# Second expert product by column halves, half of each pair's scatter and the next pair's gather inside its down stage, and a one-queue opening with idle matmuls

## The chip, the cores and the metric

One NeuronCore of one Trainium2 chip runs the kernel. The metric is the device time of a launch in microseconds (us), lower is better. TensorE (PE) multiplies, VectorE (DVE) and ScalarE (ACT) do the elementwise work and empty PSUM, GpSimd (POOL) does little, SyncE (SP) issues nearly all DMAs. SBUF holds the data, PSUM has eight banks of 128 x 512 f32 in which products are summed. Everything is float32; a matmul instruction shows in the trace as two MATMUL records, so counts in the trace are twice those of the program.

## The reference

For 256 tokens of width 1024: three token mixers (a gated linear recurrence, an mLSTM and a gated delta rule) from one input projection `x @ w_in`, merged by gates and projected; a layer norm; a mixture of 32 experts, four for each token; a second layer norm.

```python
x = layer_norm(DN_ALPHA * x + token_mixers(x, ...), ln1_g, ln1_b)
top_val, top_idx = top_k(x @ router_w + router_b, 4); gate = softmax(top_val)
# for each expert e and its tokens:
hdn = x[tok] @ w1[e] + b1[e]                     # 1024 -> 2 x 1024
act = min(glu, 7) * sigmoid(1.702 * glu) * (clip(lin, -7, 7) + 1)
y   = act @ w2[e] + b2[e]                        # 1024 -> 1024
out[tok] += gate * y
x = layer_norm(DN_ALPHA * x + out, ln2_g, ln2_b)
```

## The kernel before

**The mixers (0 to 400 us).** The input lies turned (features on partitions) in `XT`; the projection weights come as 50 pieces of 1 MB or 0.5 MB (`weight_stream`) into three buffers `WB`. Products are called `gq` (query, key, value of the delta rule), `lx`, `ly`, `mq` and so on; `proj` makes one (L589). The first, `gq0`, is in `first_proj` (L628): its input and its weights come in four quarters, the weights by SP (L403), the input by ACT (L1109), and PE begins when the first quarter of both has landed. `small` (L635) follows, then `gq1` to `gq5`. DVE begins when `planes`, a table of constants that ACT loads fifth, has landed.

**The experts (405 us to the end).** Experts are taken in 16 pairs; of each expert up to 64 tokens, so that a pair fills the 128 partitions of an output as two column tiles (`a` = 0, 1). The weights of a pair are 24 chunks of 1 MB: 8 for the first half of the hidden width (`up(0, c)`), 8 for the second (`up(1, c)`, both L972), 8 for the product back (`down(c)`, L990). SP loads them two at a time (a step, 2 MB) into eight places, and waits for `chunk_used` before it reuses one (`load_turn`, L393); steps that fit beforehand are loaded during the mixers. The last step of a pair of pairs comes in two halves (L508). What PE does besides, in a pair: `bias` (L965), `turn_hidden` (L981, after DVE's `hidden`), `turn_gates` (L999) which turns the gate-weighted one-hot table, `gather` (L902), two halves, which collects the rows of the next pair by a product with a one-hot table `ONE`, and `scatter` (L890), which adds the pair's result `YS` to the output sums in PSUM banks 4 to 7. ACT's `gathered` copies each gathered half to `XE`, and ACT and DVE each copy half of `YS`.

**The order.** It is written out by hand: each engine runs its program in order and waits on semaphores. In pair `i` before, after two chunks of the up stage PE scatters pair `i-1` (both halves), then, around chunk 4, turns the gates of pair `i` and gathers for pair `i+1`; the down stage holds chunks and `turn_hidden` alone. The first pair has the gates and the gather of pair 1 in its down stage (`prepare`). From the fifth turn on the pairs run in a loop on the device. After the last pair: ACT and DVE copy `YS`, PE scatters both halves (3.43 us), DVE makes the statistics (L1793, L1796), subtracts the mean (L1807), ACT scales (L1378), POOL adds (L560), SP stores (L524 to L528).

## Time and profile before

| | us |
|---|---|
| median of 3 runs | 1332.62 (1331.07 to 1334.09) |
| the profiled execution: its time | 1331.97 |
| its span, first to last instruction | 1330.1 |
| PE busy | 1274.4 (96%) |
| DVE busy | 341.7 (26%) |
| DMA, share of the 16 engines, 500 to 1300 us | 1.01 |
| chain that ended last: PE, DMA, DVE | 74%, 24%, 1% |

The chain is followed back from the last instruction to whatever released each step. PE's share counts an engine that is nearly always busy, so the shares alone do not tell which of PE and DMA sets the time of a stage; the stretches do.

### The profile page before, as it was taken

What the parts mean: (1) busy time and instruction counts of PE and PEld (TensorE: products, weight loads), DVE (VectorE), ACT (ScalarE), POOL (GpSimd) and SP (SyncE); (2) the same over time, 40 slices, a digit from 0 to 9 for tenths busy, and PEclk for the clock granted to TensorE, in tenths of its full rate; (3) what the DMA queues carried; (4) which work ended last, traced back from release to release, by engine and by line L of the source; (5) the groups of instructions that cost most, each with busy time, mean ns of one, the idle gap of its engine ahead of it and who ended that gap; (6) DMA issues with size and microseconds to landing.
All of it is one profiled execution on the core that took longest, in us unless ns stands there. A gap on an engine that the chain in (4) does not pass through costs nothing.

```text
span 1330.1 us, 17352 instructions
## 1 busy us (share of the span) xinstructions
PE 1274.4 (96%) x7404; PEld 697.3 (52%) x7404; DVE 341.7 (26%) x746; ACT 157.3 (12%) x267; POOL 16.4 (1%) x19
## 2 busy tenths in 40 slices
PE   8999999999999999999999989999998999999896
PEld 7888788888884444343443434334343433334342
DVE  3868571221134211211112010120211111021113
ACT  1441630011012000000000000000000000000001
POOL 0000200000000000000000000000000000000001
PEclk9999999999999999999999999999999999999998
DMA  7645225535788999999999999999999999999995
GB/s 247 227 143 150 96 98 215 187 103 180 297 354 343 406 409 427 429 424 429 427 427 427 426 429 426 427 427 426 428 428 427 431 427 427 429 429 427 428 430 233
DMA packets 48685, 463.87 MB, mean 349 GB/s; under 512 B 11568, under 2 KB 13400, under 8 KB 16888
## 3 DMA queue, kind: packets, MB, share of 16 engines
q1 hardware_dynamic: 42072, 459.19, 83.8%
q10 hardware_dynamic: 6560, 3.89, 1.0%
q8 instruction: 43, 0.70, 0.2%
q14 instruction: 10, 0.08, 0.0%
HBM read 461.60 MB, written 1.47 MB: 348 GB/s over the span
## 4 chain that ended last, share of the span: by engine, by line
PE 74%; DMA 24%; DVE 1%; issue 0%; ACT 0%; POOL 0%; POOLq 0%; SPq 0%; DVEq 0%
PE ps L972 24%; PE ps L589 20%; DMA ring<-expert_w 14%; DMA mix<-expert_w 9%; PE ps L990 8%; PE ps L890 4%; PE ps L902 4%; PE ps L965 3%; PE ps L825 2%; PE ps L607 2%; PE ps L599 1%; PE ps L981 1%; PE ps L628 1%; PE ps L999 1%; PE ps L615 0%
## 5 line engine op out<-in xcount | busy, mean ns | idle before, releaser
L972 PE MATMUL ps<-ring,mix 128*64 128x512 f32 x1536 | 343.8, 593 | 0.1
L589 PE MATMUL ps<-mix 128*128 128x256 f32 x1248 | 273.7, 380 | 2.2 <-DVE ring L1621 2.2
L589 PEld LDWEIGHTS ps<-mix 128*128 128x128 f32 x1248 | 235.7, 190 | 35.5 <-issue 3.7
L972 PEld LDWEIGHTS ps<-ring,mix 128*64 128x64 f32 x1536 | 108.2, 137 | 196.5 <-issue 191.0
L990 PE MATMUL ps<-ring,mix 128*64 128x512 f32 x752 | 171.4, 595 | 26.0 <-DMA ring<-expert_w 26.0
L990 PEld LDWEIGHTS ps<-ring,mix 128*64 128x64 f32 x752 | 53.5, 137 | 129.7 <-issue 100.8
L972 PE MATMUL ps<-mix 128*64 128x512 f32 x512 | 115.7, 594 | 3.5 <-DMA mix<-expert_w 3.2
L1913 DVE TENSOR_SCALAR mix<-ps 128x512 f32<-128x512 f32 x32 | 22.1, 692 | 374.6 <-PE ps L972 374.6
L1922 DVE COPY mix<-ps 128x512 f32<-128x512 f32 x32 | 22.1, 692 | 245.5 <-PE ps L981 245.5
L972 PEld LDWEIGHTS ps<-mix 128*64 128x64 f32 x512 | 35.9, 137 | 74.3 <-issue 66.3
L990 PE MATMUL ps<-mix 128*64 128x512 f32 x272 | 61.6, 593 | 5.3 <-DMA mix<-expert_w 5.3
L890 PE MATMUL ps<-mix 128*64 128x512 f32 x272 | 61.3, 592 | 0.8 <-DVE mix L1928 0.8
L902 PEld LDWEIGHTS ps<-mix 128*64 128x64 f32 x1024 | 57.5, 137 | 8.6 <-issue 8.6
L1361 ACT ACTIVATE mix<-mix 128x512 f32<-128x512 f32 x32 | 20.2, 630 | 348.9 <-DVE mix L1913 348.9
L902 PE MATMUL ps<-mix 128*64 128x128 f32 x1024 | 61.2, 273 | 0.0
L965 PE MATMUL ps<-mix 128*64 128x512 f32 x252 | 59.6, 592 | 0.0
L990 PEld LDWEIGHTS ps<-mix 128*64 128x64 f32 x272 | 20.8, 137 | 43.8 <-issue 42.4
L1928 DVE COPY mix<-ps 128x512 f32<-128x512 f32 x16 | 11.1, 692 | 123.5 <-PE ps L990 123.5
L890 PEld LDWEIGHTS ps<-mix 128*64 128x64 f32 x272 | 19.4, 137 | 40.0 <-issue 38.3
L981 PEld LDWEIGHTS ps<-mix 128*64 128x64 f32 x512 | 30.1, 137 | 18.3 <-issue 18.3
L1366 ACT COPY mix<-ps 128x512 f32<-128x512 f32 x16 | 9.4, 586 | 243.7 <-PE ps L990 243.7
L965 PEld LDWEIGHTS ps<-mix 128*64 128x64 f32 x252 | 18.3, 137 | 35.1 <-issue 35.1
(271 smaller groups left out, 747.4 us busy)
## 6 DMA issues: line engine op xcount, KB each, us to landing
ring<-expert_w SPq DMA_DIRECT2D x141, 2048.0 KB, 31.8
mix<-expert_w SPq DMA_DIRECT2D x39, 2048.0 KB, 33.6
mix<-stream_w SPq DMA_DIRECT2D x42, 1024.0 KB, 4.9
mix<-expert_w SPq DMA_DIRECT2D x20, 1024.0 KB, 28.5
mix<-stream_w SPq DMA_DIRECT2D x8, 512.0 KB, 3.8
ring<-expert_w SPq DMA_DIRECT2D x4, 1024.0 KB, 6.5
mix<-stream_w SPq DMA_DIRECT2D x4, 256.0 KB, 5.5
mix<-x_turned ACTq DMA_DIRECT2D x4, 256.0 KB, 6.4
```

Of the source, the lines that this page charges most:

```text
L589: ins = mm(o[:, m * S:(m + 1) * S], w[:, c, m * P:(m + 1) * P], rhs[:, c, :], start=(m == 0 and c == 0), stop=(c == nk - 1), skip_group_ch ...
L607: ins = mm(o[0:lhs.shape[-1], lo:hi], lhs, rhs, start=True, stop=True, skip_group_check=True)
L825: ins = mm(o[:, d * GW:(d + 1) * GW], MG[:, c, t * P:(t + 1) * P], w[:, c, :], start=(d == pieces[0] and c == 0), stop=(c == KD - 1), skip ...
L890: ins = mm(PS[64 * a:64 * a + 64, 4 + 2 * t + h, :], gates[:, t * P + 64 * a:t * P + 64 * a + 64], rows[:, h * 512:(h + 1) * 512], start=f ...
L902: ins = mm(PS[64 * a:64 * a + 64, bank, c * P:(c + 1) * P], X1[:, t, k:k + 64], ONE[:, t, :], start=(c == 0 and t == 0), stop=(t == NT - 1 ...
L965: mm(PS[64 * a:64 * a + 64, bank + g, :], PICK[:, 2 * g + f, a, :], B1R, start=True, stop=False, skip_group_check=True)
L972: ins = mm(PS[64 * a:64 * a + 64, bank + g, :], XE[j][:, c, 64 * a:64 * a + 64], w[:, a * D + g * 512:a * D + g * 512 + 512], start=False, ...
L981: ins = mm(PS[64 * a:64 * a + 64, bank, c * P:(c + 1) * P], HID[:, c * P + 64 * a:c * P + 64 * a + 64], ident, start=True, stop=True, skip ...
L990: ins = mm(PS[64 * a:64 * a + 64, bank + h, :], HT[:, c // 4, c % 4, 64 * a:64 * a + 64], w[:, a * D + h * 512:a * D + h * 512 + 512], sta ...
L1361: A(SIG, GLU, ACT.Sigmoid, scale=SWIGLU).then_inc(E("sig_ready"), 1)
L1913: ts(GLU, PS[:, bank, :], LIMIT, None, ALU.min).then_inc(E("glu_ready"), 1)
L1922: nc_v.tensor_copy(HT[:, n[1], :, :], PS[:, bank, :].rearrange("p (q n) -> p q n", q=4)).then_inc(E("ht_ready"), 1)
```

## The change

1. **Opening.** Input and `gq0` weights are laid together in `first_w`, four quarters of 512 KB with 4 KB rows, and all come by SP, followed by `small_w` and, with no wait, the weights of `gq1` and `gq2`; that of `gq3` waits for `planes`. ACT issues its small loads after the fourth quarter and `planes` after `small_w`. DVE fills a 128 x 128 tile `IDLE` with ones first of all, and PE multiplies it by itself eight times (`WARM`) before `first_proj`, into a bank that nothing reads.
2. **Places.** The quarters lie where half a prefetch place lay: what was loaded as one half of step 7 early is now one half of step 4, and step 7 comes whole after the last projection.
3. **`down(k)`** takes two rows of blocks for one 512-column half: chunks 0, 1 (left) and 2, 3 (right) of the first hidden half, 4, 5 (left) and 6, 7 (right) of the second. The number and shape of its matmuls and of its bytes is the same. The left half of the result is whole after chunk 5.
4. **Scatter.** The left half (`scatter_half(0)`) goes between chunks 6 and 7 of the pair's own down stage, the right half (`scatter_half(1)`) into the up stage of the next pair, after two chunks. After the last pair the right half alone is left; DVE makes the statistics of the left half before it copies the right.
5. **Gather.** `turn_gates` and both halves of `gather` go from the up stage to the down stage one pair sooner than it, around chunk 4: pair `i` turns its gates and gathers for pair `i+1` in its own down stage. This holds for the last pair, too.

```diff
+            pe.wait_ge(E("idle_ready"), 1)
+            for n in range(WARM):
+                mm(PS[:, 7, 0:P], IDLE, IDLE, start=True, stop=True, skip_group_check=True)
...
+                sp.dma_start(area(MIX, 24 + 4 * k, 1024), first_w[k]).then_inc(E(f"first_in{k}"), 16)
+            sp.dma_start(WSM, small_w).then_inc(E("wsm_in"), 16)
...
-                if n == 1:
-                    sp.wait_ge(E("first_in2"), 32)
-                if n == 2:
-                    sp.wait_ge(E("wsm_in"), 16)
+                if n == 3:
+                    sp.wait_ge(E("planes_in"), 16)
...
                 if name == "br02":
-                    load_half(PLACES[6][:, 0:2 * D], 7, 0, "steps_in6")
+                    load_half(PLACES[4][:, 2 * D:], 4, 1, "steps_in4")
...
                 if name == "br22":
-                    load_steps(4, 0, 4)
+                    load_half(PLACES[4][:, 0:2 * D], 4, 0, "steps_in4")
...
-            load_half(PLACES[6][:, 2 * D:], 7, 1, "steps_in6")
+            load_steps(7, 0, 6)
...
+            def scatter_half(h, event, each, first=False):
+
+                for t in range(NT):
+                    for a in range(2):
+                        ins = mm(PS[64 * a:64 * a + 64, 4 + 2 * t + h, :],
+                                 GTS[:, t * P + 64 * a:t * P + 64 * a + 64], YS[:, h * 512:(h + 1) * 512],
+                                 start=first, stop=False, skip_group_check=True)
...
-                def down(c, bank):
-                    w = chunk(2 * KD + c)
-                    for h in range(2):
+                def down(k, bank):
+                    w = chunk(2 * KD + k)
+                    f, h, both = k // 4, k // 2 % 2, k % 2
+                    for c in (2 * both, 2 * both + 1):
...
+                gather(0, two + 1)
                 pe.wait_ge(E("ht_ready"), 2 * i + 2)
-                for c in range(4, KF):
-                    down(c, one)
+                turn_gates(two)
+                down(4, one)
+                pe.wait_ge(E("gt_ready"), i + 1)
+                gather(1, two)
+                if first:
+                    gates_of_all()
+                down(5, one)
+                down(6, one)
...
+                pe.wait_ge(E("ys0_ready"), i + 1)
+                scatter_half(0, "acc0_done", False, first)
+                down(7, one)
...
-            pe.wait_ge(E("ys_ready"), rounds * (2 * NPAIR))
-            scatter("acc_done")
+            pe.wait_ge(E("ys1_ready"), rounds * NPAIR)
+            scatter_half(1, "acc1_done", True)
```

**PE, the end of the loop and what follows it**, the last pair's down stage. Before (`L990` down, `L981` turn_hidden, `L890` scatter):

```order
L990 MATMUL ps<-ring,mix 64x512 x12
L981 MATMUL ps<-mix 64x128 x8
L990 MATMUL ps<-ring,mix 64x512 x12
L990 MATMUL ps<-mix 64x512 x4
L959 ISA
L990 MATMUL ps<-mix 64x512 x4
L1089 ISA
L1089 COMPARE_AND_BRANCH
L1092 REGISTER_ALU
L890 MATMUL ps<-mix 64x512 x8
```

The same place now (`L1001` down, `L991` turn_hidden, `L912` gather, `L1010` turn_gates, `L900` scatter_half):

```order
L1001 MATMUL ps<-ring,mix 64x512 x4
L1071 REGISTER_ALU
L912 MATMUL ps<-mix 64x128 x16
L1010 MATMUL ps<-mix 64x128 x4
L1001 MATMUL ps<-ring,mix 64x512 x4
L912 MATMUL ps<-mix 64x128 x16
L1001 MATMUL ps<-ring,mix 64x512 x4
L1001 MATMUL ps<-mix 64x512 x4
L900 MATMUL ps<-mix 64x512 x4
L969 ISA
L1001 MATMUL ps<-mix 64x512 x4
```

Two gathers, the turned gates and half a scatter have moved in between the last five chunks; behind the loop stand four matmuls (`L900`, half a scatter) where eight stood.

**PE, the up stage of pair 1** (the second pair). Before (`L965` bias, `L972` up, `L999` turn_gates, `L902` gather):

```order
L965 MATMUL ps<-mix 64x512 x4
L972 MATMUL ps<-ring,mix 64x512 x8
L890 MATMUL ps<-mix 64x512 x8
L972 MATMUL ps<-ring,mix 64x512 x8
L999 MATMUL ps<-mix 64x128 x4
L902 MATMUL ps<-mix 64x128 x16
L972 MATMUL ps<-ring,mix 64x512 x4
L902 MATMUL ps<-mix 64x128 x16
L972 MATMUL ps<-ring,mix 64x512 x4
```

Now (`L975` bias, `L982` up, `L900` scatter_half):

```order
L975 MATMUL ps<-mix 64x512 x4
L982 MATMUL ps<-ring,mix 64x512 x8
L900 MATMUL ps<-mix 64x512 x4
L982 MATMUL ps<-ring,mix 64x512 x16
L982 MATMUL ps<-mix 64x512 x8
```

The eight chunks of the stage stand with four matmuls between them where they stood with 8 + 4 + 16 + 16.

## Rows read from the trace of the kernel before

**Rows 1.** Stretches: us, busy time of each engine (records), PEclk, DMA share, GB/s

```profile
393.00:401.00 8.00, 8.00 (x56) 7.18 (x54) 3.18 (x14) 0.96 (x2) 0.00 (x0) 1.00 0.43 136
...
478.00:482.00 4.00, 4.00 (x22) 1.38 (x20) 0.00 (x0) 0.00 (x0) 0.00 (x0) 1.00 0.85 283
...
500.00:700.00 200.00, 200.00 (x1234) 81.11 (x1230) 35.16 (x77) 12.94 (x23) 0.00 (x0) 1.00 1.01 427
700.00:1300.00 600.00, 566.82 (x3380) 225.94 (x3378) 95.17 (x204) 34.54 (x61) 0.00 (x0) 1.00 1.01 428
```

**Rows 2.** The chain that ended last, late part: start us, us, what

```profile
1264.32 3.43 PE ps L890 x16
...
1271.19 0.44 PE ps L999 x8
1271.62 1.75 PE ps L902 x32
1273.37 1.72 PE ps L972 x8
...
1278.73 30.63 DMA ring<-expert_w
```

**Rows 3.** Waits of PE, 0 to 400 us: who waited for whom, us, times, longest

```profile
PE ps L589 <- DVE ring L1621: 2.2, 1, 2.2
```

**Rows 4.** Timeline, opening: start us, us, engine, line, operation, [idle before <-releaser]

```profile
0.75 1.91 SPq L403 DMA_DIRECT2D mix<-stream_w  x4
...
5.12 9.13 PE L628 MATMUL ps<-mix 128*128 128x256 f32 x32 [5.12 <-DMA mix<-x_turned]
...
19.79 0.06 DVE L1407 MEMSET mix<- 128x1 f32 x1 [19.79 <-DMA mix<-planes]
```

**Rows 5.** The chain again, at 92 us

```profile
92.38 6.91 PE ps L589 x32
```

**Rows 6.** Stretches of the opening, PE alone: us, PE busy (records), PEclk, DMA share, GB/s

```profile
6.00:7.00 1.00, 1.00 (x4) 1.00 0.94 328
...
10.00:11.00 1.00, 1.00 (x6) 1.00 0.91 323
```

**Rows 7.** DMA issues: line, count, KB each, median us from issue to landing

```profile
mix<-stream_w SPq DMA_DIRECT2D x8, 512.0 KB, 3.8
```

**Rows 8.** Timeline of DVE at 91 us

```profile
91.18 1.29 DVE L1501 TENSOR_TENSOR ring<-ps,mix 128x512 f32<-128x512 f32 x2 [4.23 <-PE ps L615]
```

**Rows 9.** Timeline of PE in pair 1

```profile
471.46 1.92 PE L902 MATMUL ps<-mix 128*64 128x128 f32 x32
```

**Rows 10.** Timeline, last pair and end, all engines

```profile
1304.49 1.94 PE L990 MATMUL ps<-ring,mix 128*64 128x512 f32 x8 [1.15 <-DMA ring<-expert_w]
...
1306.26 1.04 PE L981 MATMUL ps<-mix 128*64 128x128 f32 x16
...
1307.13 1.89 PE L990 MATMUL ps<-ring,mix 128*64 128x512 f32 x8
...
1309.49 3.65 PE L990 MATMUL ps<-ring,mix 128*64 128x512 f32 x16 [0.47 <-DMA ring<-expert_w]
...
1316.62 0.69 DVE L1928 COPY mix<-ps 128x512 f32<-128x512 f32 x1 [8.57 <-PE ps L990]
...
1317.36 3.65 PE L890 MATMUL ps<-mix 128*64 128x512 f32 x16 [0.78 <-DVE mix L1928]
...
1318.49 0.70 DVE L1793 BATCH_NORM_STATS2 mix<-ps 128x6 f32<-128x512 f32 x1 [1.18 <-PE ps L890]
...
1320.15 0.21 DVE L1796 BATCH_NORM_AGGREGATE mix<-mix 128x2 f32<-128x12 f32 x1
...
1322.09 1.43 DVE L1793 BATCH_NORM_STATS2 mix<-ps 128x6 f32<-128x512 f32 x2 [0.15 <-DVE mix L1803]
...
1323.32 2.35 POOL L560 TENSOR_TENSOR mix<-mix 128x1024 f32<-128x1024 f32 x1 [1172.67 <-ACT mix L1378]
...
1326.12 1.10 POOL L560 TENSOR_TENSOR mix<-mix 128x384 f32<-128x384 f32 x1 [0.46 <-ACT mix L1378]
```

More of the change, by code:

```diff
@@ L883, in _, with scatter @@
             out_proj("wo11b", 1, 1, (1,), count_first)
-            def scatter(event, gates=GTS, rows=YS, first=False):
+            def scatter(event, gates, rows):
                 for t in range(NT):
@@ L891, in scatter @@
                                      gates[:, t * P + 64 * a:t * P + 64 * a + 64], rows[:, h * 512:(h + 1) * 512],
[L892 to L894 removed]
+                                     start=False, stop=False, skip_group_check=True)
+                        ins.then_inc(E(event), 1)
+            def scatter_half(h, event, each, first=False):
[4 more added lines that the diff above has]
+                                 start=first, stop=False, skip_group_check=True)
+                    if event and (each or t == NT - 1):
+                        ins.then_inc(E(event), 1)
             def gather(half, bank):
@@ L1041, in pair @@
                     if second:
-                        pe.wait_ge(E("bank_free5"), bank_total[5])
-                        pe.wait_ge(E("gt_ready"), 1)
-                        pe.wait_ge(E("xe_ready"), 4)
-                    pe.wait_ge(E("ys_ready"), 2 * i)
-                    scatter(None, first=second)
-                    up(0, 2, one)
-                    up(0, 3, one)
-                if not first:
-                    pe.wait_ge(E("xe_ready"), 2 * i + 2)
-                    turn_gates(two)
-                    pe.wait_ge(E("onehot"), i + 2)
-                    gather(0, two + 1)
-                    up(0, 4, one)
-                    pe.wait_ge(E("gt_ready"), i + 1)
-                    gather(1, two)
-                    for c in range(5, KD):
+                        for b in (5, 7):
+                            pe.wait_ge(E(f"bank_free{b}"), bank_total[b])
+                    pe.wait_ge(E("ys1_ready"), i)
+                    scatter_half(1, None, False, second)
+                    for c in range(2, KD):
                         up(0, c, one)
-                    pe.wait_ge(E("xe_ready"), 2 * i + 4)
                 bias(1, two)
@@ L1106, in _ @@
             A = nc_s.activation
-            for k in range(QUARTERS):
-                first, last = KD // QUARTERS * k, KD // QUARTERS * (k + 1)
-                act.dma_start(XT[:, first:last, :], x_turned[:, first:last, :]).then_inc(E(f"first_in{k}"), 16)
-            act.dma_start(WSM, small_w).then_inc(E("wsm_in"), 16)
+            act.wait_ge(E(f"first_in{QUARTERS - 1}"), 16)
             act.dma_start(VC, vectors).then_inc(E("vec_in"), 16)
             act.dma_start(SC[:, 32:34], row_bias).then_inc(E("bias_in"), 16)
-            act.wait_ge(E(f"first_in{QUARTERS - 1}"), 16)
+            act.wait_ge(E("wsm_in"), 16)
             act.dma_start(CM, planes.rearrange("p (k n) -> p k n", n=P)).then_inc(E("planes_in"), 16)
@@ L1356, in turn_act @@
                     first = isinstance(i, int) and i == 0
-                    if not first:
-                        prepared(i, 1 - j, (two, two + 1, two))
                     for f in range(2):
```

106 lines of the change are left out of this document (50 added, 56 removed).

## The prediction, written before the changed kernel ran

> **What bounds the kernel now.** I read the stretches first, then the chain, then the timeline at three places: the opening, pairs 0 and 1, and the end. The stretches show three regimes [rows 1]. Up to 400 us PE is busy nearly all the time and the DMAs are not. From 500 to 700 us both are full: PE 200.00 of 200, DMA share 1.01 at 427 GB/s. From 700 us on PE has gaps (566.82 of 600) and the DMAs have none (1.01, 428 GB/s). So in the expert stage the weights decide: PE needs less for a pair than the DMAs do. A chunk of 1.049 MB at 427.6 GB/s is 2.45 us, a pair of 24 chunks 58.9 us. PE's pair is 24 chunks at 1.72, two biases at 1.72, a scatter of 3.43, two gathers at 1.75, gates 0.44 and two turns of the hidden values at 0.87 (1306.26 to 1307.13): 53.8 us [rows 2, 10]. Up to 700 us PE eats what was loaded beforehand, then it waits for each step. The chain says the same: one of its last pieces is a DMA of 30.63 us, up to the middle of the last down stage [rows 2].
>
> Two things follow. PE work saved or moved inside a pair in the middle is worth nothing. The end comes as: the time at which the stream of loads starts to run full, plus bytes over rate, plus every stretch in which the load queue runs dry, plus what stands after the last loads. The change is priced at these four.
>
> **The opening.** The stream runs full from about 405 us, when PE begins to free places, so what PE wins in the mixers moves everything behind it. PE starts at 5.12 and `first_proj` takes 9.13 us for 32 records [rows 4]; the same 32 records elsewhere take 6.91 [rows 5]. The stretches tell why: 4 records touch a microsecond from 6 to 7, and 6 from 10 to 11 [rows 6]. PEclk reads 1.00 in both, so the column does not show it; the pace of the records does: first the lower level (1.2 GHz), later the upper (2.4). A record of 256 columns takes 6.91/32 = 0.216 us on the upper, 0.43 on the lower, so 9.13 us are about 10 slow records and 22 fast ones: 4.4 us of work at the lower level, 2.2 us lost.
>
> The ones: 8 matmuls, 16 records of half the columns, 0.215 us each if slow, 3.4 us. They need only DVE's fill, so I estimate a start at 1.0 us (the first DMAs are issued at 0.75) and an end at 4.4. The first quarter, 512 KB on one queue, is of a size that lands 3.8 us after issue in the stream [rows 7]: 4.55 instead of 5.12, a gain of 0.57. If the rise comes 4.4 us after the first matmul, as it did, it comes at 5.4, and 0.85 us of `first_proj` runs slow, losing 0.43 instead of 2.2. The opening gains 0.57 + 2.2 - 0.4 = **2.3 us**. The bounds: 0, if the clock stays low and the input comes no sooner; 2.8, if none of it is slow. I stand near the upper end because the measured slow stretch has a length that the ones nearly fill. The data keeps up: quarters 1.2 us apart against 1.7 us of PE work each.
>
> Here a rule speaks against a part of it. In the trace, input and weights come on two queues and land at 5.12. By the Trainium skill (DMA: Bandwidth & Descriptors, "Queues, rings and completion order") each DMA engine takes turns between the queues, packet by packet, so two queues share the same engines. By that the first 512 KB take as long on one queue as on two, the 0.57 is gone, and the sum would be 0.6 us higher.
>
> Does the gain reach 405 us? PE waits little before 400 us, its longest wait being 2.2 us for a DVE chain that PE itself started [rows 3]. The one chain with a start of its own is DVE's, which begins when `planes` lands at 19.79 [rows 4] and is at 91.18 idle for 4.23 us waiting for PE [rows 8]. `planes` now goes behind `small_w` and beside `gq1` and `gq2`, and no longer beside `gq3`; less stands ahead of it, and I expect it 1 to 3 us earlier. With 4.23 us of slack even no change would do. So all 2.3 us arrive.
>
> **Places.** One MB moves from before the last projection to behind it, 2.45 us of transfer. From 393 to 401 us the DMA share is 0.43 at 136 GB/s [rows 1]: some 4.5 us are free there. Nothing.
>
> **Where the queue runs dry.** From 478 to 482 us the DMAs move 283 GB/s [rows 1]: (428 - 283) x 4 / 428 = 1.4 us of stream lost. The cause is PE: in pair 1, around the gather at 471.46 us, it does a scatter, gates and two gathers (3.43 + 0.44 + 1.75 + 1.75) with only three chunks between them [rows 2, 9], so places come free too slowly while few loads are queued. In the change the gather and gates for pair 2 and half the scatter are gone from that stage: 1.72 + 0.44 + 3.5 = 5.7 us less between its chunks; pair 0 takes 1.72 us more (the left scatter before its last chunk). Net, the places of that stage come free up to 3.9 us sooner, more than the 1.4 us of hole. **-1.4 us.** Bounds: 0, if the hole only moves into pair 1's down stage, where the gathers now stand; -2.9, if slow stretches near it close too. I take the hole as measured.
>
> **The middle.** PE's work of a pair is the same 53.8 us under 58.9. The new waits are covered: the left half of `YS` is copied during chunk 6 (1.72 us against 0.78 from the end of a product to the scatter's start [rows 10]), the gates during chunk 4. Later releases in the down stage delay SP by at most 5.7 us, while its queue is some 30 us deep [rows 2]. Nothing.
>
> **The end.** This is the term that speaks against the change. The second step of the last down stage lands at 1304.49, the next at 1309.49 [rows 10]. Before, PE then has chunks 2 to 7 (6 x 1.72) and a turn (0.87), 11.2 us, and 0.5 us of waits: done at 1316.4, the copy at 1316.62. Now between chunks 3 and 7 stand also two gathers (useless in the last pair, but issued), gates and the left scatter: 2 x 1.75 + 0.44 + 1.72 = 5.7 us. They fill the 0.47 us gap before 1309.49 and little else: 1304.49 + 11.2 + 5.7 = 1321.4, **5.0 us later**.
>
> Behind it: copy (0.69) and scatter start, 1317.36 before, 1322.36 now. First statistics 1.13 us after the scatter's start as before (1318.49). Before, two statistics (0.92 apart) came before the aggregate at 1320.15; now one, the left having been made while PE ran chunk 7: 1322.36 + 1.13 + 0.70 + 0.03 = 1324.2, 4.1 us later. For the second block of rows one statistic of 0.7 us is saved again, 3.4 us later. POOL adds the first block for 2.35 us from 1323.32 + 4.1 and begins the second behind it, at 1329.8 instead of 1326.12. **+3.7 us.** Bounds: +3.4 (POOL no matter), +5.0 (no saving in the statistics, if DVE's left ones delay its copy).
>
> **The sum**, against the profiled execution (span 1330.1, time 1331.97): -2.3 - 1.4 + 3.7 = 0.0, which on the median of 1332.62 gives 1332.6. Two gains and one loss cancel.
>
> **The rivals.**
> 1. The clock is not ready: between the last ones (4.4) and the first quarter PE is idle, and if the clock stays on its lower level until some 4 us after the input starts, only the earlier input is left, 0.57. For it: the ones are shorter than the slow stretch measured. Against: the gap is short. Sum: 3.7 - 1.4 - 0.6 = +1.7, 1334.3. Chance 0.2.
> 2. Slower: `planes` lands late. It is on ACT's queue behind waits for the fourth quarter and `small_w`, with 2 MB of `gq1` and `gq2` already queued on SP's. DVE's slack of 4.2 us is cut by PE's gain of 2.3; if `planes` lands after 21.7, DVE at 91.18 holds PE, and each further microsecond costs one. At 25 us it costs 3.3 and the result is 1335.9. Against: before, it landed at 19.79 with more bytes beside it. Chance 0.1. The nearest neighbour, a hole that stays in pair 1 together with an unprofitable opening, gives +3.1, chance 0.07.
> 3. Faster: the last pair's extra work is hidden, because PE is more often idle for data there than the trace shows. PE's waits in that down stage after chunk 3 are 0.5 us, so most of 5.0 can't hide; if the last loads landed 3 us later against PE's work, the end would cost 0.7 instead of 3.7: 1329.6. Or both gains reach their bounds (2.8 + 2.9): 1330.6. Chance together 0.15.
> 4. The change does not do what it says, the ones not running before the input: PE would do them after its data is there, and lose up to 3.4: 1338. Against: their only wait is for DVE's fill. Chance 0.01.
>
> **The numbers.** My forecast has 0.47: 1332.6, between 1331.2 and 1334. The range of 8 in 10 takes in rival 1 and reaches into 2 and 3: 1329.5 to 1336. 0.2% is 2.7 us, about what a measurement here can tell from no change. Faster than 1329.9: 0.13 (the far side of rival 3). Slower than 1335.3: 0.17 (rival 2 and neighbour, and the tail at its upper bound with rival 1). Within: 0.70.
>
> **What would show it.** In the opening: `first_proj` starting near 4.6 and lasting 7.3. PE's first chunk 2.3 us earlier. No stretch under 400 GB/s at 470 to 485 us. The last DVE copy of `YS` 7 us, not 2, after the last expert load. `first_proj` at 9 us refutes the ones; a hole in the pair 1 down stage refutes the second gain; a last copy less than 4 us after the last load refutes the price of the end.

## The result, and the profile after

| | before | changed |
|---|---|---|
| median of 20 runs each, us | 1332.34 (1330.87 to 1334.53) | 1334.02 (1333.36 to 1335.06) |
| the profiled execution: time, span | 1331.97, 1330.1 | 1334.72, 1332.9 |
| PE busy | 1274.4 | 1278.7 |

Ratios and counts of executions here and below leave out a single one of the kernel before, of 2263 us at a mean granted clock of 0.556. The ratio is 1.0014, 95% interval 1.0008 to 1.0020: the change costs 1.9 us (1.1 to 2.7). The forecast was 0.0 us, with a range of 1329.5 to 1336. The time lies inside the range, but the interval excludes no change: the balance of two gains and one loss didn't come out even.

The same places as in the rows of before. The opening [rows 4], timeline of the changed kernel (start us, us, engine, line, operation, [idle before <-releaser]):

```profile
0.84 0.17 DVE L1404 MEMSET mix<- 128x128 f32 x1 [0.84 <-PEq L2020]
1.06 3.79 PE L631 MATMUL ps<-mix 128*128 128x128 f32 x16 [1.06 <-DVE mix L1404]
...
4.74 8.24 PE L626 MATMUL ps<-mix 128*128 128x256 f32 x32
12.82 3.62 PE L636 MATMUL ps<-mix,ring 128*128 128x256 f32 x16
...
17.75 0.06 DVE L1406 MEMSET mix<- 128x1 f32 x1 [16.74 <-DMA mix<-planes]
```

The ones (L631) run from 1.06 and `first_proj` (L626) follows without a gap, 0.38 us sooner than before and 0.89 us shorter. `small` (L636) starts at 12.82, against 14.08 before: 1.26 us gained, not 2.3. `planes` is there at 17.75 instead of 19.79, so rival 2 is out.

The stretches [rows 1], all engines:

```profile
478.00:482.00 4.00, 4.00 (x22) 1.30 (x20) 2.67 (x4) 0.63 (x1) 0.00 (x0) 1.00 1.04 442
500.00:700.00 200.00, 200.00 (x1232) 81.37 (x1230) 33.90 (x75) 12.54 (x23) 0.00 (x0) 1.00 1.01 427
700.00:1300.00 600.00, 564.63 (x3370) 222.70 (x3368) 96.28 (x205) 33.55 (x61) 0.00 (x0) 1.00 1.01 428
```

The hole of 283 GB/s at 478 us is closed, and the middle is as before. The end [rows 10]:

```profile
1303.22 1.94 PE L1001 MATMUL ps<-ring,mix 128*64 128x512 f32 x8 [1.15 <-DMA ring<-expert_w]
...
1304.99 1.04 PE L991 MATMUL ps<-mix 128*64 128x128 f32 x16
...
1305.86 1.89 PE L1001 MATMUL ps<-ring,mix 128*64 128x512 f32 x8
...
1307.58 1.92 PE L912 MATMUL ps<-mix 128*64 128x128 f32 x32
...
1309.32 0.61 PE L1010 MATMUL ps<-mix 128*64 128x128 f32 x8
...
1311.48 1.92 PE L912 MATMUL ps<-mix 128*64 128x128 f32 x32
...
1316.66 1.89 PE L900 MATMUL ps<-mix 128*64 128x512 f32 x8
...
1320.31 0.69 DVE L1927 COPY mix<-ps 128x512 f32<-128x512 f32 x1 [0.28 <-PE ps L1001]
...
1326.08 3.88 POOL L559 TENSOR_TENSOR mix<-mix 128x1024 f32<-128x1024 f32 x2 [1176.71 <-ACT mix L1376]
...
1327.52 1.59 DVE L1961 SCALAR_TENSOR_TENSOR mix<-mix 128x640 f32<-128x640 f32 x1 [0.15 <-DVE mix L1802]
```

From the start of the first chunk of the second step to the last DVE copy of `YS` it is 1320.31 - 1303.22 = 17.09 us, before 1316.62 - 1304.49 = 12.13. The two gathers (L912), the gates (L1010) and the left scatter (L900) stand between the last chunks, and PE doesn't wait once between these two points. The loads end before: the stretch from 1314 to 1315 us moves 49 GB/s, the next none, so the copy comes 5.3 us behind the last load. The forecast named 7, and "less than 4" as its refutation.

**The account** needs a place that the forecast had not named. PE's longest wait before 400 us [rows 3] ends at 183.13 us in the changed kernel and at 184.41 before; it is called the pause at 181 us below. What follows it differs (stretches, PE alone: us, PE busy (records), PEclk, DMA share, GB/s):

```profile
182.00:183.00 1.00, 0.00 (x0) 1.00 0.00 0
183.00:184.00 1.00, 0.87 (x4) 1.00 0.00 0
184.00:185.00 1.00, 1.00 (x6) 0.72 0.00 0
185.00:186.00 1.00, 1.00 (x4) 0.50 0.00 0
186.00:187.00 1.00, 1.00 (x4) 0.50 0.00 0
187.00:188.00 1.00, 1.00 (x4) 0.58 0.00 0
```

PE resumes at 183.13 us after 2.17 us without work. Soon after, its granted clock falls to 0.50, the lower level (1.2 GHz), and is back at 1.00 at 188 us. The timelines give the price, changed kernel first, then the kernel before:

```profile
183.13 15.74 PE L588 MATMUL ps<-mix 128*128 128x256 f32 x64 [2.17 <-DVE ring L1620]
```

```profile
184.41 14.05 PE L589 MATMUL ps<-mix 128*128 128x256 f32 x64 [2.18 <-DVE ring L1621]
```

The same 64 records take 15.74 us instead of 14.05: 1.69 us lost. So the two profiled executions differ by:

| stretch | before | changed | difference | forecast |
|---|---|---|---|---|
| start to `small` | 14.08 | 12.82 | -1.26 | -2.3 |
| `small` to PE's first up chunk | 393.99 | 395.66 | +1.67 | 0 |
| first up chunk to the last pair's second down step | 896.42 | 894.74 | -1.68 | -1.4 |
| that step to the last DVE copy of `YS` | 12.13 | 17.09 | +4.96 | +5.0 |
| that copy to the end of the span | 13.48 | 12.59 | -0.89 | -1.3 |
| sum | 1330.1 | 1332.9 | +2.8 | 0.0 |

### The profile page after: what moved, and what is told of

Same layout as the page of the kernel before. It is cut to its first block, busy times and chain, and to the rows that moved or that the text cites. A ratio compares the mean times of both kernels' runs of the same rounds, so it can differ in the third digit from the quotient of the medians.

```text
span 1332.9 us, 17354 instructions
## 1 busy us (share of the span) xinstructions
PE 1278.7 (96%) x7420; PEld 698.8 (52%) x7420; DVE 342.1 (26%) x747; ACT 155.8 (12%) x267; POOL 16.8 (1%) x19
## 4 chain that ended last, share of the span: by engine, by line
PE 75%; DMA 23%; DVE 1%; ACT 0%; issue 0%; POOL 0%; POOLq 0%; SPq 0%; DVEq 0%
DMA ring<-expert_w 23%; PE ps L588 21%; PE ps L982 18%; PE ps L1001 14%; PE ps L912 4%; PE ps L900 4%; PE ps L975 3%; PE ps L826 2%; PE ps L607 2%; PE ps L991 1%; PE ps L599 1%; PE ps L626 1%; PE ps L1010 1%; PE ps L615 0%; PE ps L802 0%
## 5 line engine op out<-in xcount | busy, mean ns | idle before, releaser
L982 PE MATMUL ps<-ring,mix 128*64 128x512 f32 x1536 | 341.4, 594 | 12.3 <-DMA ring<-expert_w 12.2
L982 PEld LDWEIGHTS ps<-ring,mix 128*64 128x64 f32 x1536 | 107.8, 137 | 230.4 <-issue 202.6
L1001 PE MATMUL ps<-ring,mix 128*64 128x512 f32 x752 | 175.0, 594 | 15.9 <-DMA ring<-expert_w 15.9
L982 PE MATMUL ps<-mix 128*64 128x512 f32 x512 | 115.5, 593 | 1.9 <-DMA mix<-expert_w 1.9
L1001 PEld LDWEIGHTS ps<-ring,mix 128*64 128x64 f32 x752 | 51.9, 137 | 99.5 <-issue 80.2
L982 PEld LDWEIGHTS ps<-mix 128*64 128x64 f32 x512 | 36.2, 137 | 71.6 <-issue 67.9
L1001 PE MATMUL ps<-mix 128*64 128x512 f32 x272 | 63.0, 593 | 6.6 <-DMA mix<-expert_w 6.6
L912 PEld LDWEIGHTS ps<-mix 128*64 128x64 f32 x1024 | 58.1, 137 | 18.3 <-issue 18.3
L912 PE MATMUL ps<-mix 128*64 128x128 f32 x1024 | 61.3, 273 | 0.0
L900 PE MATMUL ps<-mix 128*64 128x512 f32 x256 | 60.4, 592 | 0.8 <-DVE mix L1927 0.8
L975 PE MATMUL ps<-mix 128*64 128x512 f32 x252 | 59.6, 592 | 0.0
L1001 PEld LDWEIGHTS ps<-mix 128*64 128x64 f32 x272 | 20.1, 137 | 46.0 <-issue 46.0
L1336 ACT COPY mix<-ps 128x512 f32<-128x512 f32 x32 | 18.8, 586 | 205.4 <-PE ps L912 205.4
L991 PEld LDWEIGHTS ps<-mix 128*64 128x64 f32 x512 | 30.2, 137 | 18.3 <-issue 18.3
L900 PEld LDWEIGHTS ps<-mix 128*64 128x64 f32 x256 | 18.3, 137 | 37.7 <-issue 36.0
L975 PEld LDWEIGHTS ps<-mix 128*64 128x64 f32 x252 | 18.0, 137 | 35.5 <-issue 35.4
```

The costliest lines, as they stand in the source:

```text
L900: ins = mm(PS[64 * a:64 * a + 64, 4 + 2 * t + h, :], GTS[:, t * P + 64 * a:t * P + 64 * a + 64], YS[:, h * 512:(h + 1) * 512], start=first ...
L912: ins = mm(PS[64 * a:64 * a + 64, bank, c * P:(c + 1) * P], X1[:, t, k:k + 64], ONE[:, t, :], start=(c == 0 and t == 0), stop=(t == NT - 1 ...
L975: mm(PS[64 * a:64 * a + 64, bank + g, :], PICK[:, 2 * g + f, a, :], B1R, start=True, stop=False, skip_group_check=True)
L982: ins = mm(PS[64 * a:64 * a + 64, bank + g, :], XE[j][:, c, 64 * a:64 * a + 64], w[:, a * D + g * 512:a * D + g * 512 + 512], start=False, ...
L991: ins = mm(PS[64 * a:64 * a + 64, bank, c * P:(c + 1) * P], HID[:, c * P + 64 * a:c * P + 64 * a + 64], ident, start=True, stop=True, skip ...
L1001: ins = mm(PS[64 * a:64 * a + 64, bank + h, :], HT[:, f, c, 64 * a:64 * a + 64], w[:, a * D + c % 2 * 512:a * D + c % 2 * 512 + 512], star ...
```

## The experiments

The main theory: the end costs what was forecast (5.7 us of PE work in a down stage that has hardly any time to spare), the gather out of pair 1's up stage closes the hole, and only the opening fails, because the clock falls after the pause at 181 us. On that fall two theories compete: it comes **with the ones**, or it comes **by chance** from execution to execution. A rival on the stream: the hole was worth nothing, and the shorter stream is **noise** of one execution. All kernels compute the whole reference. Since one execution turned out to say little of the opening, the table collects the quantities of the account in every profile; each section below uses its rows. "Stream" is the time from PE's first up chunk to the last pair's second down step, "step to copy" the time from there to the last DVE copy of `YS`. "Filled" means that PE had work in the pause, and no fall came behind it.

| kernel | `small` starts | clock falls after the pause | first up chunk | stream | step to copy | copy to end | span |
|---|---|---|---|---|---|---|---|
| before | 14.08 | no | 408.07 | 896.42 | 12.13 | 13.48 | 1330.1 |
| b1_before_again | 14.97 | no | 408.95 | 895.28 | 12.11 | 13.56 | 1329.9 |
| b3_before_third | 14.81 | no | 408.79 | 895.57 | 12.12 | 13.52 | 1330.0 |
| e1_opening | 12.75 | no | 406.73 | 895.47 | 12.11 | 13.49 | 1327.8 |
| a3_opening_again | 11.94 | yes | 407.61 | 895.71 | 12.12 | 13.56 | 1329.0 |
| e2_pairs | 14.31 | no | 408.28 | 894.66 | 17.09 | 12.57 | 1332.6 |
| changed | 12.82 | yes | 408.48 | 894.74 | 17.09 | 12.59 | 1332.9 |
| a1_changed_again | 11.59 | yes | 407.25 | 895.08 | 17.09 | 12.58 | 1332.0 |
| a2_changed_third | 12.81 | no | 406.79 | 894.69 | 17.09 | 12.63 | 1331.2 |
| e3_no_ones | 13.85 | no | 407.82 | 894.93 | 17.09 | 12.56 | 1332.4 |
| b2_no_ones_again | 14.59 | yes | 410.20 | 894.16 | 17.08 | 12.66 | 1334.1 |
| e4_filled | 12.47 | filled | 408.12 | 894.60 | 17.09 | 12.59 | 1332.4 |
| e5_gather_up | 12.06 | yes | 407.72 | 895.08 | 13.83 | 12.57 | 1329.2 |
| e6_up_filled | 12.84 | filled | 406.83 | 894.85 | 13.84 | 12.58 | 1328.1 |
| e7_whole_scatter | 11.49 | yes | 407.15 | 894.60 | 15.37 | 13.58 | 1330.7 |
| e8_all_up | 12.56 | yes | 408.22 | 897.83 | 13.83 | 12.6 | 1332.5 |
| e9_left_first | 11.69 | filled | 405.67 | 895.54 | 12.12 | 13.37 | 1326.7 |

From the start of `small` to the first up chunk the table gives 393.97 to 393.99 us in the nine profiles whose clock stayed at 1.00 in between, and 395.61 to 395.67 us in the eight where it fell once (the seven with "yes", and e4_filled, whose fall came later, see below). Nothing else between these points moves by more than 0.06 us: one fall costs 1.7 us, and all of it arrives at the first up chunk.

Measured times (medians) beside the kernel before on the same chip:

| kernel | us | ratio to before, 95% interval |
|---|---|---|
| e1_opening | 1331.04 | 0.9994 (0.9985 to 1.0003) |
| e2_pairs | 1334.22 | 1.0019 (1.0010 to 1.0028) |
| e3_no_ones | 1334.38 | 1.0018 (1.0009 to 1.0027) |
| e4_filled | 1333.09 | 1.0012 (1.0003 to 1.0021) |
| e5_gather_up | 1330.67 | 0.9995 (0.9986 to 1.0004) |
| e6_up_filled | 1329.93 | 0.9989 (0.9980 to 0.9998) |
| e7_whole_scatter | 1333.37 | 1.0014 (1.0005 to 1.0023) |
| e8_all_up | 1331.57 | 1.0003 (0.9994 to 1.0012) |
| e9_left_first | 1329.00 | 0.9980 (0.9969 to 0.9990) |
| a1_changed_again | 1334.23 | 1.0017 (1.0006 to 1.0027) |
| b1_before_again | 1331.69 | 1.0006 (0.9995 to 1.0016) |

### The two halves of the change

**e1_opening** is the kernel before with parts 1 and 2 of the change alone:

```diff
+            pe.wait_ge(E("idle_ready"), 1)
+            for n in range(WARM):
+                mm(PS[:, 7, 0:P], IDLE, IDLE, start=True, stop=True, skip_group_check=True)
...
+                sp.dma_start(area(MIX, 24 + 4 * k, 1024), first_w[k]).then_inc(E(f"first_in{k}"), 16)
```

> The kernel before with the opening of the change alone (one-queue quarters, ones, places), pairs as before. Theory A (the opening is worth its shorter first product, and the fall of the clock after the 2.2 us pause at 181 us is an accident of the single execution): about 1.3 us faster than before, 1331.0. Theory B (the shifted opening puts the pause where the clock falls, in every execution): the 1.3 us are given back, 0 to +0.4 us. A profile in which first_proj ends near 13.0 instead of 14.25 is expected by both; A expects that some executions show the granted clock at 0.5 after the pause and some do not.

**e2_pairs** is the kernel before with parts 3 to 5 alone:

```diff
+                gather(0, two + 1)
...
+                turn_gates(two)
                 down(4, one)
+                gather(1, two)
...
                 down(6, one)
+                scatter_half(0, "acc0_done", False, first)
                 down(7, one)
```

> The kernel before with the change inside the pairs alone (column halves, half scatter, gather in the down stage), opening as before. By the profile of the changed kernel: the stream of loads gains 1.4 to 1.7 us by the closed hole at 478 us, the end costs 5.0 - 0.9 = 4.1, so +2.4 to +2.7 us, 1334.9. Should it be under +1, the end is cheaper than I read, or the hole worth more.

The opening alone gains 0.8 us with zero inside its interval (0.9994); the pairs alone cost 2.5 us (1.3 to 3.7). In e2's profile the end is that of the changed kernel to 0.02 us (17.09 and 12.57), its stream is short (894.66) and its opening that of before. So all of the loss is in the pairs part, where its expectation (2.4 to 2.7) had it, and the opening pays back less than the forecast's 2.3.

### The ones and the pause

**e3_no_ones** is the changed kernel without the ones:

```diff
-            pe.wait_ge(E("idle_ready"), 1)
-            for n in range(WARM):
-                mm(PS[:, 7, 0:P], IDLE, IDLE, start=True, stop=True, skip_group_check=True)
...
-            nc_v.memset(IDLE, 1.0).then_inc(E("idle_ready"), 1)
```

> The changed kernel without the ones. A: the clock rises later against first_proj, which then takes about 9.1 us from 4.6 to 4.7 us on; about 1 us slower than the changed kernel, 1335.0. If the ones do nothing (the rise comes at a time of its own), the same as the changed kernel, 1334.0.

**e4_filled** is the changed kernel with ten idle products in the pause at 181 us. They wait for an earlier tile (`c0`) of the chain for which PE pauses, so that they stand inside the pause:

```diff
+            moved(pe, "c0")
+            for n in range(10):
+                mm(PS[:, 4, 0:P], CM[:, K_ONES], CM[:, K_ONES], start=True, stop=True, skip_group_check=True)
             fill(4)
```

> The changed kernel with ten matmuls of 128 columns on constants put into PE's pause at 181 to 183 us, in a PSUM bank that is free there (2.15 us of work, nothing reads it). A: where the clock fell (3.4 us at 0.5, 1.7 us lost), it no longer falls; the spread of the times narrows and the median falls by 1.7 times the share of executions with the fall, 0.5 to 1. B: the full 1.7 us, 1332.3. If the clock is not what the pause costs: no change, or up to 0.5 us slower by the fill itself.

Without the ones PE has no work until the input, and `first_proj` takes longer (timeline of PE, e3_no_ones):

```profile
4.54 9.47 PE L626 MATMUL ps<-mix 128*128 128x256 f32 x32 [4.54 <-DMA mix<-first_w]
```

Two things follow. The input is there at 4.54 us in both profiles without ones (e3, b2), and at 4.93 to 5.12 in the four with the opening of before: the new loads bring it 0.5 us sooner on average. By the Trainium skill (DMA: Bandwidth & Descriptors, "Queues, rings and completion order") queues share the engines in turns, and by that rule one queue alone should have won nothing. No run here tests it, since the rows grew from 2 KB to 4 KB at the same time: from 2 to 5 us the DMAs move 333 and 329 GB/s (e3, b2) against 240 before, and whether the queue or the rows did that stays open. And the ones are what shortens `first_proj`: 9.47 and 10.21 us without them, 7.07 to 8.37 in the eleven profiles with them. In the time this can't be seen: e3's ratio is 1.0018 against 1.0014, and its expectation of 1 us more is neither met nor refuted.

In e4_filled the records after the filled pause take 14.05 us again (timeline of PE):

```profile
180.45 2.40 PE L747 MATMUL ps<-mix 128*128 128x128 f32 x20
182.79 14.05 PE L588 MATMUL ps<-mix 128*128 128x256 f32 x64
```

But its first up chunk is at 408.12, since here the clock was low at another place, and PE was busy all the time before it (stretches, PE alone):

```profile
392.00:396.00 4.00, 4.00 (x36) 0.95 0.98 317
396.00:400.00 4.00, 4.00 (x15) 0.62 0.28 113
```

Its ratio, 1.0012, can't be told from the changed kernel's 1.0014. The expectation that the spread of the times narrows failed: they run from 1331.85 to 1334.70 us, those of the changed kernel from 1333.36 to 1335.06. Filling this pause takes away this fall, not every fall. After these four both theories of the fall were alive: it had come once with ones (changed), not with ones in e1, and not without them in e3.

### Each kernel once more

Whether the fall belongs to the kernel or to the execution can only be seen by repeating. a1_changed_again and a2_changed_third are the changed kernel unaltered, a3_opening_again is e1, b2_no_ones_again is e3, b1_before_again and b3_before_third are the kernel before. a2, a3, b2 and b3 are single executions, read for their profiles alone.

> The changed kernel again, for its profile. If the fall of the clock after the pause at 181 us goes with the opening that has the ones (seen in 4 of 5 profiles with them and an unfilled pause, in none of 3 without), it is there again, and PE's first chunk comes at 408.0 to 408.5; if it is chance, it may be missing, and the first chunk then comes near 406.7.

> The kernel before again, for its profile. If the fall goes with the ones: no fall, first chunk near 408.1. If it is chance: in about every second profile a fall, first chunk near 409.8.

> The changed kernel a third time, for its profile. So far the clock fell after the pause at 181 us in 5 of 6 profiles of kernels with the ones and an unfilled pause, in 0 of 4 without the ones. If it goes with the ones: a fall, first chunk 407.2 to 408.5. If it is chance: even odds.

> The kernel before with the new opening, again: the one profile with the ones in which the clock did not fall. If it goes with the ones: a fall this time, first chunk near 408. If this kernel escapes it for a reason of its own: none again, first chunk near 406.7.

> The changed kernel without the ones, again. If the fall goes with the ones: none, first chunk near 407.8. If chance: even odds.

> The kernel before a third time. If the fall goes with the ones: none, first chunk 408 to 409. If chance: even odds.

The third execution of the changed kernel kept its clock (stretches, PE alone), where the first lost it:

```profile
182.00:183.00 1.00, 0.00 (x0) 1.00 0.00 0
183.00:184.00 1.00, 0.87 (x4) 1.00 0.00 0
184.00:188.00 4.00, 4.00 (x21) 1.00 0.00 0
```

and the second execution without ones lost it, where the first did not:

```profile
184.00:185.00 1.00, 0.09 (x1) 0.90 0.00 0
185.00:186.00 1.00, 1.00 (x3) 0.50 0.00 0
186.00:187.00 1.00, 1.00 (x4) 0.50 0.00 0
187.00:188.00 1.00, 1.00 (x3) 0.50 0.00 0
188.00:189.00 1.00, 1.00 (x6) 0.89 0.00 0
```

e1 and a3, too, are one kernel with both outcomes, as theory A of e1 had it. So the fall is not fixed by the kernel; it changes from execution to execution. Over all profiles with an unfilled pause it came in 6 of 8 with ones (changed, a1, a3, e5, e7, e8; not e1, a2) and in 1 of 6 without (b2; not before, b1, b3, e2, e3); where the pause was filled, in 0 of 3. The profiles are few, but every execution of the experiments has its mean granted clock on record, and so have the twenty of the changed kernel. The mean also counts the end, where PE has no more work and its clock falls in every profile (0.50 from 1328 us on in the changed kernel). In the profiles a mean of 0.998 never goes with a fall (a2, b1, b3, e2, e3), one of 0.996 always does (a1, a3, e5), and 0.997 goes with either.

| executions with an unfilled pause | number | mean clock 0.996 or less | 0.998 |
|---|---|---|---|
| with ones | 74 | 35 | 4 |
| without ones | 123 | 8 | 98 |

The times go along: of the kernel before on the chip of e1, the three executions at 0.996 took 1333.63 to 1333.97 us, where those at 0.998 took 1331.56 on average. So far as the mean stands for the fall, it is much more frequent with the ones: both theories hold a part. Filling the pause helps only in part: of 30 such executions (e4, e6, e9) 5 have 0.996 or less and 9 have 0.998. How the opening reaches 170 us ahead is not shown. The table of the profiles gives a hint: with ones and an unfilled pause, the five in which `small` starts earliest (11.49 to 12.56) all have the fall, and of the three between 12.75 and 12.82 one has it.

The opening itself varies as well. Timeline of PE, a1_changed_again:

```profile
1.06 3.65 PE L631 MATMUL ps<-mix 128*128 128x128 f32 x16 [1.06 <-DVE mix L1404]
4.58 7.17 PE L626 MATMUL ps<-mix 128*128 128x256 f32 x32
11.59 3.62 PE L636 MATMUL ps<-mix,ring 128*128 128x256 f32 x16
```

Here `first_proj` takes 7.17 us, near the forecast's 7.3, where the changed kernel's first profile shows 8.24. So a1 has the fall and yet its first up chunk at 407.25, sooner than the 408.0 expected with a fall. With ones `small` starts at 12.27 on average of 11 profiles (11.49 to 12.84), with the opening of before (before, b1, b3, e2) at 14.54 of 4 (14.08 to 14.97). The mean gain is 2.27 us: 0.40 by the earlier start of `first_proj` (4.64 against 5.04 us on average) and 1.87 by its shorter run (7.80 against 9.67). The forecast's 2.3 was right on average, and the profile of before was the most favourable of its four executions.

### The gather, and the hole in pair 1

**e5_gather_up** is the changed kernel with the gates and both gathers back in the up stage, but in the pairs of the device loop alone; the eight pairs ahead of the loop (four turns of two), pair 1 among them, keep them in the down stage:

```diff
+                early = not isinstance(turn, int)
...
+                    if early:
+                        turn_gates(two)
+                        pe.wait_ge(E("onehot"), i + 2)
+                        gather(0, two + 1)
+                    up(0, 4, one)
+                    if early:
+                        pe.wait_ge(E("gt_ready"), i + 1)
+                        gather(1, two)
...
-                gather(0, two + 1)
+                if not early:
+                    gather(0, two + 1)
```

> The changed kernel, but in the loop (pairs 8 to 15) the gates and the gather stand in the up stage again, around chunk 4, as before the change; pairs 0 to 7 keep them in the down stage; column halves and half scatters everywhere. Theory A (the end costs what PE issues between chunks 3 and 7 of the last pair): from the landing of the last pair's second down step to the last copy of YS 17.1 - 3.9 + 0.5 (the wait for the next step comes back) = 13.6 us; the stream unchanged; 3.5 us faster than the changed kernel, some 1.7 us faster than before. Rival (the end is long because of the half scatter before the last chunk): only 0 to 1 us faster than the changed kernel.

**e6_up_filled** is e5 with the filled pause of e4.

> The one with the gather back in the up stage of the loop, plus ten matmuls in PE's pause at 181 us. If the clock falls after that pause in a share of the executions, its median is 0.3 to 1 us below that of the same kernel without the fill, and no execution shows the clock under 1 between 184 and 188 us.

**e8_all_up** is e5 with the gathers in the up stage of every pair but the first, pair 1 too:

```diff
-                early = not isinstance(turn, int)
+                early = not (isinstance(i, int) and i == 0)
```

> As the one with the gather in the up stage of the loop, but in all pairs from pair 1 on. A (the hole in the stream is made by the gather in pair 1's up stage): a stretch under 350 GB/s between 474 and 484 us is back, the time from PE's first chunk to the landing in the last pair is 1.4 us longer than where the gather stands in pair 1's down stage (896.1 against 894.7). If it is the scatter alone that made the hole, which is halved here: no hole, no difference.

The last pair of e5 (timeline of PE):

```profile
1302.80 1.94 PE L1001 MATMUL ps<-ring,mix 128*64 128x512 f32 x8 [1.15 <-DMA ring<-expert_w]
...
1307.78 3.65 PE L1001 MATMUL ps<-ring,mix 128*64 128x512 f32 x16 [0.45 <-DMA ring<-expert_w]
1311.24 1.92 PE L1001 MATMUL ps<-mix 128*64 128x512 f32 x8
1312.96 1.91 PE L900 MATMUL ps<-mix 128*64 128x512 f32 x8
1314.67 1.91 PE L1001 MATMUL ps<-mix 128*64 128x512 f32 x8
```

Step to copy is 13.83 us, 3.26 less than 17.09. The 3.94 us of gathers and gates are gone, and the wait for the next step is back: from step to step it is 4.98 us (1302.80 to 1307.78) where two chunks and a turn take 4.36 (1303.22 to 1307.58 in the changed kernel), so 0.62 us are lost again, more than the 0.45 that the row shows. 3.94 - 0.62 = 3.32. The time follows: its ratio of 0.9995 stands against 1.0014, 2.5 us less; the expectation said 3.5, and the intervals of both ratios leave room for that. The rival that only the half scatter makes the end long (0 to 1 us) is refuted by the 3.26. The price of the end is confirmed in the profile. e6's median is 0.7 us below e5's, as expected, with intervals that overlap.

e5 and e8 show the hole, one with the gather of pair 1 in the down stage, one with it in the up stage (stretches, PE alone, e5 first):

```profile
478.00:482.00 4.00, 4.00 (x22) 1.00 1.01 430
```

```profile
474.00:478.00 4.00, 4.00 (x44) 1.00 1.00 426
478.00:482.00 4.00, 4.00 (x22) 1.00 0.80 279
482.00:500.00 18.00, 18.00 (x98) 1.00 1.00 422
```

With the gather back in pair 1's up stage, 279 GB/s are back at 478 us, at the very place where the kernel before has 283. All profiles agree: from 474 to 486 us the DMAs move 350 to 382 GB/s in the six with the gather in pair 1's up stage (before, b1, b3, e1, a3, e8), and 415 to 425 in the eleven others. Among these are e7 and e9 (421 and 425), which have the whole scatter there and not the gather, so the scatter alone doesn't make the hole. The cause of the hole was named rightly, and the noise theory falls as to the mechanism. The size at its place is right, too: (421 - 368) x 12 / 428 = 1.5 us on average. What reaches the length of the stream is less certain. e8's stream is 2.75 us longer than e5's, where its hole by itself is 1.5 us of bytes. Over all profiles, the five with the whole pair of before (before, b1, b3, e1, a3) have a stream of 895.69 us on average (895.28 to 896.42), the nine with the pair 1 of the change (changed, a1, a2, e2, e3, b2, e4, e5, e6) 894.75 (894.16 to 895.08): the change is worth 0.94 us there, and where the other half microsecond goes is not shown. What makes e8's difference to e5 so much larger than its hole stays open, and its median, 1331.57, is only 0.9 us above e5's, with overlapping intervals.

### The half scatter

**e7_whole_scatter** is the changed kernel with no scatter before the last chunk: both halves go into the next pair's up stage, and after the last pair comes the whole scatter, with the statistics of before:

```diff
+                    pe.wait_ge(E("ys0_ready"), i)
+                    scatter_half(0, None, False, second)
                     pe.wait_ge(E("ys1_ready"), i)
                     scatter_half(1, None, False, second)
...
-                pe.wait_ge(E("ys0_ready"), i + 1)
-                scatter_half(0, "acc0_done", False, first)
                 down(7, one)
```

> The changed kernel, but both halves of the scatter stand in the next pair's up stage and after the last pair, as before the change; column halves and the gather in the down stage stay. A: the last copy of YS comes 1.7 us sooner, 15.4 us after the step's landing; behind it the end is 0.9 us longer (two statistics for each block of rows again); so 0.8 us faster than the changed kernel, 1.1 us slower than before. If the half scatter pays, it is slower than the changed kernel.

The copy comes 15.37 us after the step, 1.72 less than 17.09: half a scatter, to the hundredth. Behind it 13.58 us are left instead of 12.59: about 1 us given back, since the statistics of the left half are no longer made ahead. The half scatter thus costs 1.72 us in front of the copy and brings 0.9 to 1.0 behind it, a net loss of 0.7 to 0.8. The times can't tell a difference of that size: both ratios are 1.0014.

**e9_left_first** puts together what the others left standing: e6, with both scatter halves in the next pair's up stage, and after the last pair the left scatter while DVE still copies the right half:

```diff
+            pe.wait_ge(E("ys0_ready"), rounds * NPAIR)
+            scatter_half(0, "acc0_done", True)
             pe.wait_ge(E("ys1_ready"), rounds * NPAIR)
             scatter_half(1, "acc1_done", True)
```

> The kernel with the gather in the up stage of the loop and the filled pause, and with both halves of the scatter in the next pair's up stage; after the last pair PE scatters the left half first, while DVE still copies the right half, and DVE makes the left statistics behind its copy. From the landing of the second down step to the last copy 12.1 us (13.8 less 1.72); from the copy to the end 13.5 or a little less, the left scatter now standing in the 0.78 us in which PE waited for the copy. In sum 1.0 us less than with the half scatter before the last chunk: 1329.0, ratio to before about 0.998. If the half scatter inside the stage is worth its place, it is no faster than that kernel.

Timeline of its end (PE and DVE):

```profile
1301.21 1.94 PE L1004 MATMUL ps<-ring,mix 128*64 128x512 f32 x8 [1.14 <-DMA ring<-expert_w]
...
1313.09 3.63 PE L903 MATMUL ps<-mix 128*64 128x512 f32 x16
...
1313.33 0.69 DVE L1953 COPY mix<-ps 128x512 f32<-128x512 f32 x1 [8.56 <-PE ps L1004]
1314.19 0.70 DVE L1818 BATCH_NORM_STATS2 mix<-ps 128x6 f32<-128x512 f32 x1 [0.17 <-PE ps L903]
```

PE runs the whole scatter (L903) without a gap behind its last chunk, the copy falls into its left half, and the statistics begin 0.86 us after the copy's start, before 1.87 (1318.49 - 1316.62). Of this 1.0 us only 0.15 arrive at the end (13.37 against 13.52 from the copy on), since three statistics now stand before the first aggregate where two stood: it comes 3.37 us after the copy's start (1316.70 - 1313.33), before 3.53. Step to copy is 12.12 us as before, and with the filled pause and the ones its time is 1329.0: 0.9980 (0.9969 to 0.9990) of the kernel before, 2.7 us faster than it and, by the two ratios, 4.5 us faster than the changed kernel. It beats both. Against e6 (0.9989) the intervals overlap; in the profiles its step to end is 0.93 us shorter (25.49 against 26.42), as expected, and its first up chunk, at 405.67 against 406.83, was the luckier.

## Why the prediction was right or wrong

**The end, right where it was largest.** "1304.49 + 11.2 + 5.7 = 1321.4, 5.0 us later": measured 4.96, and the same 17.09 us in six profiles, 17.08 in a seventh. e5 and e7 take its parts away one by one (3.26 and 1.72). The work between the last chunks, counted from rows of before, was nearly the whole price; this stage has 0.6 us of waits to give and no more, so rival 3 had no footing. One reading was loose: "11.2 us, and 0.5 us of waits" from 1304.49 make 1316.2 and not 1316.4, because the wait from step to step is 0.64 us (5.00 - 4.36), not 0.47. It changes nothing of note.

**Behind the copy, mechanism right, size off by 0.4.** Forecast -1.3, measured -0.89. POOL's first addition starts 2.76 us later than before (1326.08 against 1323.32) where the copy is 3.69 later: the 0.9 us of statistics. The second follows at once, as forecast. But the forecast gave the second its old 1.10 us, and it takes 1.58 (timeline of POOL, changed kernel, from 1328.5 us on):

```profile
1328.38 1.58 POOL L559 TENSOR_TENSOR mix<-mix 128x384 f32<-128x384 f32 x1
```

DVE's last addition (L1961) now starts while POOL's first one still runs and ends inside its second, and takes 1.59 us instead of 0.89 itself (last section). All eleven profiles in which POOL runs its two additions without a gap show the same (1.57 to 1.58 and 1.59 us), the other six 1.10 to 1.11 and 0.88 to 0.89. So 0.48 us of the saving are lost again.

**The hole, right in cause, too large in effect.** -1.4 forecast; the hole itself is 1.5 us, but the stream is shorter by 0.94 over many profiles. The two first profiles gave -1.68, because the profile of before had the longest stream of the five with its pairs. "No stretch under 400 GB/s at 470 to 485" held: from 474 to 486 us e2_pairs moved at least 406.

**The opening, where the prediction failed.** The step is "So all 2.3 us arrive". 2.27 us were won by the start of `small`, on average. At the first up chunk, the profiles with ones and an unfilled pause stand at 407.49 on average (8), those with the opening of before at 408.52 (4): 1.03 us. The missing 1.2 us are the clock after the pause at 181 us, 1.69 us in 6 of 8 profiles (1.27 on average) against none of those four. In the profiles without a fall the gain does arrive: `small` to first up chunk is 393.98 us with ones (e1, a2) as without. The forecast had this pause in its rows [rows 3] and counted it as a wait of 2.2 us that moves with PE; that the clock can fall behind it was put at nothing. It could not be seen in the profile of before, which kept its clock. Rival 1 had "the clock is not ready" as a cause, with +1.7 us and 1334.3, close to the time measured, but at another place: in the opening itself the clock rises at varying times and costs nothing on average against the forecast. That 1334.3 came so near is luck.

**The sum.** -1.03 (opening as it arrives) - 0.94 (stream) + 4.96 - 0.92 (end, averages of the profiles with either pair) = +2.07 us, measured +1.9 (1.1 to 2.7). Forecast 0.0: about 1.3 us of the miss are the opening, 0.5 the stream, 0.4 the additions. The averages are of few profiles, so the agreement with the time is no finer than some tenths of a microsecond.

**Rivals 2 and 4** are refuted by `planes` at 17.75 and the ones at 1.06.

## What to carry to other kernels

Work that a pipeline hides in its middle must be priced again at its last turn: there two gathers and the gates, whose results nothing needs, cost 3.3 of their 3.9 us, and what is well placed in the first pairs may be ill placed in the last. Read an early gain through to the place where it is spent, pause by pause, and look at the granted clock after each pause of PE; and take a term of 1 or 2 us from several profiles, with the mean clock of every execution beside them, since the start of `small` alone ranged over 0.9 us in the kernel before and 1.2 in the changed one.

## What the runs showed of the hardware

- **After a pause of 2.2 us PE's clock can halve.** In 7 of 14 profiles the granted clock went from 1.00 to 0.50 as PE resumed or up to 1.3 us later, for some 3.4 us; 64 records took 15.74 us instead of 14.05. With work in the pause it never fell there (0 of 3), and the same kernel showed both.
- **It can fall with PE busy.** In e4_filled PEclk is 0.95 from 392 to 396 us and 0.62 from 396 to 400, with PE busy 4.00 of 4 in both; just before, PE ran 28 records of only 32 columns and two of 128 (392.06 to 395.3). The same work stands there in every kernel, and in the sixteen other profiles the clock stayed at 1.00.
- **The opening's low clock is not in the column.** PEclk reads 1.00 from 6 to 7 us [rows 6], though the records run at half pace; after the pause it reads 0.50 for the same pace.
- **POOL and DVE slow each other.** DVE's `SCALAR_TENSOR_TENSOR` of 128 x 640, two inputs from SBUF, takes 1.59 us where POOL's additions run beside all of it, and 0.89 before, where they cover half of it (0.44 us); POOL's addition of 384 columns takes 1.58 instead of 1.10, the one of 1024 columns 2.35 in both. The Trainium skill (GPSIMD Engine Reference, "Specifications") says that GpSimd's SBUF interfaces are shared with VectorE and contend with its instructions that have two SBUF inputs; the trace agrees.
- **The loads' rate is steady.** 427 or 428 GB/s from 500 to 1300 us in both kernels; what the order changes is the few microseconds around it.
